# The opening of a two-network fp32 kernel: modulation by four column chunks, the first two value heads in plain fp32

## The chip, the cores and the metric

One core of a Trainium2 chip runs the kernel. The metric is the device time of one execution in microseconds (us), median of several runs. The engines are TensorE (PE), VectorE (DVE), ScalarE (ACT), GpSimd (POOL) and SyncE (SP), which here issues all transfers.

## What is computed

Two small networks of two layers each, 512 tokens by 1024 features in fp32. The change touches only the start of the first layer:

```
cond = silu(c)
mod = cond @ ada_w[l] + ada_b[l]
shift, scale, gate = split(mod, 3)
h = x * (1 + scale) + shift
proj = h @ w_in                       # u, v, z_a, x_b, z_b, 1024 columns each
v = layer_norm(v per head of 256 columns, norm_g, norm_b)
sv = einsum('hts,bnshd->bnthd', masked ws, v)   # "spatial" product, per head
a = u * (sv + b) * silu(z_a)
...                                   # pooling branch, output product, three more layers
```

## The kernel before

The weights `wt` lie in tiles T of 128 by 2048 numbers (1 MB). ACT rounds a tile to fp32r (`w_hi`, `split_tile`), DVE takes the rest (`w_lo`), and every large product is three fp32r matmuls (`mm3`: low by high, high by low, high by high). The modulated input is split in the same way into `h_hi` and `h_lo`, eight blocks k of 128 features. Tiles T = 0 to 3 are the value heads h = 0 to 3 ("V"), each in two chunks of one PSUM bank (c = 0, 1, two token blocks each); T = 4 and on are U, Z, ZB, XB and the rest. For each V chunk ACT copies the bank to `tmp`, and DVE normalizes it into `vn` ("post": statistics, reciprocal, scaling). `spatial(h)` multiplies `vn` of head h by `ws` into banks 4 and 5, from which DVE makes `park`; the next spatial product may only overwrite a bank when `park` of the one before has been read out of it (`sv_taken`).

A unit is one of shift, scale, gate of a layer. Its columns are the sum over eight pieces k (128 rows of `adat`, 1024 columns, 512 KB each) of `cond[k]` times the piece, which DVE adds up in `acc`; PE then sums over the partitions by multiplying with `ones`, one column a matmul. In the opening, units 0 (shift) and 1 (scale) are needed before `h` exists. All 16 pieces, `ada_first`, are fetched first, pieces 1 and 3 go straight through PE (`first_mods`, L1024), and scale is done in two halves. `keep_busy` multiplies constants for no result. `wb[T]` is the weight buffer of a tile, `before_in[T]` the tile that was in it. One pair of buffers takes all tiles but three.

All orders are written out by hand: `plan_steps` makes one list of steps, each engine walks it, and counting semaphores tie them. SP issues transfers in its own order and waits where a buffer is in use. DVE also adds a piece of a later unit (`ada_piece`) in each tile, fetched into `ada_raw` by halves of 64 rows.

## Time and profile before

| | |
|---|---|
| median of 3 runs | 1363.78 us (1362.84 to 1364.08) |
| the profiled execution | 1363.42 us |
| its span | 1361.6 us |
| PE busy | 1327.5 us, 97% of the span |
| DVE busy | 912.9 us, 67% |
| ACT busy | 563.5 us, 41% |

The span is what the trace covers; the execution's time is 1.8 us more. Busy time of PE is modelled for pipelined matmuls, so it tells where PE has work, not how fast it is.

### The profile page before, as it was taken

What the parts mean: (1) busy time and instruction counts of PE and PEld (TensorE: products, weight loads), DVE (VectorE), ACT (ScalarE), POOL (GpSimd) and SP (SyncE); (2) the same over time, 40 slices, a digit from 0 to 9 for tenths busy, and PEclk for the clock granted to TensorE, in tenths of its full rate; (3) what the DMA queues carried; (4) which work ended last, traced back from release to release, by engine and by line L of the source; (5) the groups of instructions that cost most, each with busy time, mean ns of one, the idle gap of its engine ahead of it and who ended that gap; (6) DMA issues with size and microseconds to landing.
All of it is one profiled execution on the core that took longest, in us unless ns stands there. A gap on an engine that the chain in (4) does not pass through costs nothing.

```text
span 1361.6 us, 17379 instructions
## 1 busy us (share of the span) xinstructions
PE 1327.5 (97%) x6761; PEld 1123.4 (83%) x6761; DVE 912.9 (67%) x1325; ACT 563.5 (41%) x851; POOL 303.3 (22%) x204
## 2 busy tenths in 40 slices
PE   5999999999999999999999999999999999999997
PEld 5998888778888878888888788888888888888885
DVE  5754544774486568988678786686776577676553
ACT  1423222221254246666422475543342566534430
POOL 0200200064420015555344100001116200011123
PEclk9999999999999999999999999999999999999998
DMA  9654443323424422213344243313314322211111
GB/s 378 187 165 139 139 140 141 136 94 139 147 93 140 132 74 63 70 36 93 94 139 140 93 158 118 96 48 139 135 51 161 118 93 78 78 63 62 62 63 62
DMA packets 31378, 155.14 MB, mean 114 GB/s; under 512 B 4160, under 2 KB 4288, under 8 KB 20032
## 3 DMA queue, kind: packets, MB, share of 16 engines
q1 hardware_dynamic: 31296, 154.03, 33.5%
q8 instruction: 54, 0.88, 0.3%
q14 instruction: 28, 0.23, 0.1%
HBM read 151.92 MB, written 2.10 MB: 113 GB/s over the span
## 4 chain that ended last, share of the span: by engine, by line
PE 87%; DVE 6%; issue 3%; ACT 3%; DMA 1%; SPq 0%; POOL 0%; DVEq 0%; ACTq 0%; POOLq 0%
PE bank L838 25%; PE bank L840 24%; PE bank L839 24%; PE bank L845 1%; PE bank L1302 1%; PE bank L992 1%; PE bank L1136 1%; PE bank L1276 1%; DVE acc L1669 1%; PE bank L1278 1%; PE bank L974 1%; DMA ada_first<-adat 1%; PE bank L1123 1%; PE bank L1140 1%; DVE qn_lo L1928 1%
## 5 line engine op out<-in xcount | busy, mean ns | idle before, releaser
L838 PE MATMUL bank<-h_lo,w_hi 128*128 128x512 f32 x1008 | 397.5, 394 | 1.5 <-DVE h_lo L1805 1.0
L840 PE MATMUL bank<-h_hi,w_hi 128*128 128x512 f32 x1008 | 392.8, 390 | 0.0
L839 PE MATMUL bank<-h_hi,w_lo 128*128 128x512 f32 x1008 | 392.4, 389 | 0.0
L1628 DVE TENSOR_TENSOR w_lo<-w_raw,w_hi 128x2048 fp32r<-128x2048 f32 (+2 forms) x91 | 207.1, 2276 | 85.6 <-ACT w_hi L1347 85.5
L838 PEld LDWEIGHTS bank<-h_lo,w_hi 128*128 128x128 f32 x1008 | 189.3, 188 | 41.1 <-issue 3.5
L840 PEld LDWEIGHTS bank<-h_hi,w_hi 128*128 128x128 f32 x1008 | 189.2, 188 | 40.0
L839 PEld LDWEIGHTS bank<-h_hi,w_lo 128*128 128x128 f32 x1008 | 189.4, 188 | 38.2 <-issue 0.5
L1347 ACT ACTIVATE w_hi<-w_raw 128x2048 fp32r<-128x2048 f32 (+2 forms) x91 | 166.7, 1832 | 86.0 <-PE bank L840 77.8
L1423 ACT ACTIVATE tmp<-bank 128x512 f32<-128x512 f32 x48 | 28.6, 595 | 124.4 <-PE bank L840 115.0
L2214 POOL TENSOR_SCALAR q_dup<-rot_y 128x512 fp32r<-128x512 f32 x8 | 11.9, 1492 | 302.7 <-DVE rot_y L1680 302.7
L1669 DVE SCALAR_TENSOR_TENSOR acc<-ada_raw,cond_pair,acc 128x1024 f32<-128x1024 f32 x45 | 58.5, 1300 | 0.0
L838 PE MATMUL bank<-mixc_lo,w_hi 128*128 128x512 f32 x128 | 50.6, 396 | 0.0
L840 PE MATMUL bank<-mixc_hi,w_hi 128*128 128x512 f32 x128 | 49.9, 390 | 0.0
L839 PE MATMUL bank<-mixc_hi,w_lo 128*128 128x512 f32 x128 | 49.8, 389 | 0.0
L2128 DVE TENSOR_TENSOR_SCAN keep<-keep 128x127 f32<-128x127 f32 (+2 forms) x64 | 49.0, 807 | 0.4
L2227 POOL TENSOR_TENSOR sum<-sum,sqr 128x512 f32<-128x512 f32 x24 | 48.0, 2001 | 1.9
L1764 DVE SCALAR_TENSOR_TENSOR x<-bank,gate,x 128x512 f32<-128x512 f32 x16 | 12.0, 751 | 50.5 <-PE bank L840 50.4
L2305 POOL TENSOR_TENSOR rope_t<-qr_f,sin 32x512 f32<-32x512 f32 x28 | 37.9, 1353 | 33.2 <-ACT qr_f L1562 30.7
L2226 POOL TENSOR_TENSOR sqr<-x 128x512 f32<-128x512 f32 x24 | 37.5, 1560 | 23.8 <-DVE x L1774 22.7
L1669 DVE SCALAR_TENSOR_TENSOR acc<-ada_raw,cond,acc 128x1024 f32<-128x1024 f32 x28 | 41.1, 1469 | 0.0
L2214 POOL TENSOR_SCALAR mixc_hi<-sz 128x512 fp32r<-128x512 f32 x16 | 23.9, 1492 | 76.0 <-DVE sz L1914 76.0
L2214 POOL TENSOR_SCALAR mixa_hi<-park 128x512 fp32r<-128x512 f32 x8 | 11.9, 1492 | 124.4 <-DVE park L1737 124.4
(349 smaller groups left out, 2675.0 us busy)
## 6 DMA issues: line engine op xcount, KB each, us to landing
w_raw<-wt SPq DMA_DIRECT2D x83, 1024.0 KB, 6.0
ada_raw<-adat SPq DMA_DIRECT2D x96, 256.0 KB, 4.0
ada_raw<-adat SPq DMA_DIRECT2D x32, 512.0 KB, 3.6
ada_first<-adat SPq DMA_DIRECT2D x16, 512.0 KB, 12.4
w_raw<-wt SPq DMA_DIRECT2D x8, 640.0 KB, 5.2
spare_raw<-wt SPq DMA_DIRECT2D x3, 1024.0 KB, 5.9
x<-xt SPq DMA_DIRECT2D x4, 512.0 KB, 15.5
out<-outf SPq DMA_DIRECT2D x8, 256.0 KB, 2.2
```

What stands on the lines that cost most here:

```text
L838: pe.matmul(dst, ah, bl, start=start, stop=False, skip_group_check=True)
L839: pe.matmul(dst, al, bh, start=False, stop=False, skip_group_check=True)
L840: return pe.matmul(dst, ah, bh, start=False, stop=stop, skip_group_check=True)
L1347: act.activation(w_hi[wb[T]][:, 0:n], w_raw[wb[T]][:, 0:n], ACT.Copy).then_inc(w_hi_done, 1)
L1423: act.activation(dst, src, func, scale=scale, bias=bias).then_inc(chunk_taken, 1)
L1628: dve.tensor_tensor(w_lo[wb[T]][:, 0:n], w_raw[wb[T]][:, 0:n], f(w_hi[wb[T]][:, 0:n]), ALU.subtract).then_inc(w_lo_done, 1)
L1669: dve.scalar_tensor_tensor(acc[:, g % 2, :], src, c, acc[:, g % 2, :], ALU.mult, ALU.add).then_inc(ada_done, 1)
L2128: ins = dve.tensor_tensor_scan(k, k, k, 1.0, ALU.mult, ALU.min)
L2214: return pool.tensor_scalar(dst, src, 1.0, None, ALU.mult)
L2226: link(pool.tensor_tensor(sqr[:], x[:, n, :], x[:, n, :], ALU.mult))
L2227: ins = pool.tensor_tensor(sum2[:], sum2[:], sqr[:], ALU.add)
L2305: pool.tensor_tensor(rope_t[to, :], qr_f[of, :], sin1[of, :], ALU.mult).then_inc(qr_turned, 1)
```

## The change

The two units of the opening are fetched by four chunks of 256 columns each, both units in one transfer: 32 pieces of 256 KB in place of 16 of 512 KB. After each chunk DVE and PE make the columns of two blocks k, ACT makes `h_first` (plain fp32) and from it `h_hi`, and PE multiplies the two blocks for value heads 0 and 1 at once in fp32, with the weights as they landed (`first_values`; four banks, one for each chunk of output). So tiles 0 and 1 are not split. Tiles 2 and 3 land in buffers of their own (`early_raw`). The direct pieces, `keep_busy` in the opening and POOL's copy of `h` go. The spatial product of head 0 moves from behind head 1 to between the two chunks of head 2, that of head 1 stays behind head 2. `splits(T)` counts the split tiles, in place of T + 1 everywhere. The diff, cut to its core:

```diff
--- before.py
+++ after.py
@@ -139,10 +139,12 @@
     for h in range(GH):
         T = begin()
         chunk("V", T, h=h, c=0)
+        if h == 2:
+            steps.append(dict(op="spatial", h=0))
         chunk("V", T, h=h, c=1)
         if h == 0:
             steps.append(dict(op="spatial_rows"))
-        else:
+        elif h >= 2:
             steps.append(dict(op="spatial", h=h - 1))
         after_tile(T)
...
@@ -478,6 +488,9 @@
             w_hi.append(place(f"spare_hi{i}", [P, TILE], F32R, o + 8 * KB))
             w_lo.append(place(f"spare_lo{i}", [P, TILE], F32R, o + 16 * KB))
+        for i in range(2):
+            w_raw.append(place(f"early_raw{i}", [P, TILE], F32, area + (16 + 8 * i) * KB))
...
@@ -698,6 +714,8 @@
         def split_with(T):
+            if T < 3:
+                return [3] if T == 1 else []
...
@@ -739,6 +757,8 @@
         for d in kinds:
             aside = d["kind"] in ("AV", "AG") and d["u"] == 0 or d["kind"] == "QC" and d["n"] >= 2 or d.get("aside")
             bk = CHUNK_BANK[d["C"]] = (2 + d.get("sub", 0)) if aside else 2 if d is OUT0_FIRST else d["C"] % 2
+            if d["C"] in OPENING:
+                bk = CHUNK_BANK[d["C"]] = d["C"]
             BEFORE_IN_BANK[d["C"]] = last_in.get(bk, -1)
...
@@ -775,20 +795,39 @@
         @block.sync
         def _(sp):
             sp.dma_start(cols[:], colst).then_inc(cols_in, 16)
-            sp.dma_start(w_raw[0][:], wt[0]).then_inc(w_landed[0], 16)
-            for i in range(2 * SEC):
-                sp.dma_start(ada_first[:, i, :], adat[i]).then_inc(ada_first_landed[i], 16)
-                if i == 0:
-                    sp.dma_start(mats[:], matst).then_inc(const_in, 16)
-                    sp.dma_start(rmats_raw[:], rmatst).then_inc(rmats_in, 16)
-            for i in range(4):
+            def first_chunk(c):
+                for k in range(SEC):
+                    cut = slice(FIRST_COLS * c, FIRST_COLS * (c + 1))
+                    sp.dma_start(ada_first[:, c, k], adat[k:SEC + k + 1:SEC, :, cut].rearrange("u p d -> p u d")
+                                 ).then_inc(ada_first_landed[SEC * c + k], 16)
+            def first_x(i):
                 sp.dma_start(x[:, 2 * i:2 * i + 2, :], xt[:, 2 * i:2 * i + 2, :]).then_inc(x_landed[i], 16)
-            sp.dma_start(w_raw[1][:], wt[1]).then_inc(w_landed[1], 16)
+            def first_weights(T):
+                sp.dma_start(w_raw[raw_of[T]][:], wt[T]).then_inc(w_landed[raw_of[T]], 16)
+            first_chunk(0)
+            sp.dma_start(mats[:], matst).then_inc(const_in, 16)
+            first_weights(0)
+            first_x(0)
+            first_weights(1)
+            for c in range(1, FIRST_CHUNKS):
+                first_chunk(c)
+                if c == FIRST_CHUNKS - 1:
+                    sp.wait_ge(ada_done, 2 * SEC)
+                    first_weights(2)
+                first_x(c)
             sp.dma_start(ws[:], wst).then_inc(layer0_in, 16)
             sp.dma_start(bs[:], bst).then_inc(layer0_in, 16)
+            sp.dma_start(rmats_raw[:], rmatst).then_inc(rmats_in, 16)
+            first_weights(3)
             for T in range(NT):
-                if before_in[T] >= 0:
-                    sp.wait_ge(w_lo_done, before_in[T] + 1)
+                if raw_before[T] >= 2:
+                    sp.wait_ge(w_lo_done, splits(raw_before[T]))
+                elif raw_before[T] >= 0:
+                    wait_tile_done(sp, raw_before[T])
                 if 2 <= before_in[T] - head_tile <= MH // 2:
                     sp.wait_ge(uv_lo_done, before_in[T] - head_tile - 1)
                 if T == spare_tiles[0]:
@@ -799,8 +838,8 @@
                 elif T == spare_tiles[2]:
                     sp.wait_ge(ro_full, RH)
                 n = cols_of[T]
-                if T >= 2:
-                    sp.dma_start(w_raw[wb[T]][:, 0:n], wt[T, :, 0:n]).then_inc(w_landed[wb[T]], 16)
+                if T >= 4:
...
@@ -1015,37 +1035,49 @@
                                   h_hi[:, k, :], h_lo[:, k, :], i == 0, i == DC - 1)
                 ins.then_inc(chunk_full, 1)
...
+            def first_columns(c):
+                pe.wait_ge(ada_done, SEC * (c + 1))
+                if c >= 2:
+                    pe.wait_ge(first_cols, c - 1)
+                for u in range(2):
+                    for j in range(FIRST_COLS // P):
+                        a = FIRST_COLS * c + P * j
+                        i = u * FIRST_COLS // P + j
+                        ins = pe.matmul(bank[:, 6 + c % 2, i:i + 1], acc[:, u, a:a + P], ones[:, 0:1],
+                                        start=True, stop=True)
+                ins.then_inc(first_full, 1)
+            def first_values(k, h):
+                pe.wait_ge(h_v_done, k + 1)
+                if k == 0:
+                    pe.wait_ge(w_landed[raw_of[h]], 16)
+                for c in range(2):
+                    for i in range(2):
+                        blk = slice((2 * c + i) * P, (2 * c + i + 1) * P)
+                        ins = pe.matmul(bank[:, 2 * h + c, i * HD:(i + 1) * HD], h_first[:, k, blk],
+                                        w_raw[raw_of[h]][:, k * HD:(k + 1) * HD], start=i == 0 and k == 0,
+                                        stop=k == DC - 1, skip_group_check=True)
+                    if k == DC - 1:
+                        ins.then_inc(chunk_full, 1)
+            def opening():
                 pe.wait_ge(const_in, 16)
...
+                first_columns(0)
+                for k in range(DC):
+                    first_values(k, 0)
+                    if k in (3, 5):
+                        first_columns((k + 1) // 2)
+                    first_values(k, 1)
+                    if k == 1:
+                        first_columns(1)
             def head_qr(j):
                 T = head_tile + j
...
+                pe.wait_ge(w_lo_done, splits(T))
                 if j == 0:
                     pe.wait_ge(qk_lo, 4)
                 if j == 1:
...
@@ -1424,14 +1458,11 @@
             act.wait_ge(cols_in, 16)
             act.activation(cond[:], col("c", 0, 16), ACT.Silu).then_inc(cond_done, 1)
-            split_tile(0)
             act.wait_ge(cond_done, 1)
             for e in range(2):
                 for i in range(2):
                     act.activation(cond_pair[64 * e:64 * e + 64, :, i], cond[64 * i:64 * i + 64, :],
                                    ACT.Copy).then_inc(cond_pair_done, 1)
-            act.wait_ge(rmats_in, 16)
-            act.activation(rmats[:].rearrange("p a b -> p (a b)"), rmats_raw[:], ACT.Copy).then_inc(masks_done, 1)
             v_count = 0
             for d in steps:
                 op = d["op"]
@@ -1454,11 +1485,20 @@
                                    bias=eps_ln[:] if d["mean"] else eps_rho[:] if d["lhs"] == "derived" else
                                    col("eps", d["eps"])).then_inc(sts_done, 1)
                 elif op == "h" and d["l"] == 0:
-                    for k in range(DC):
-                        act.wait_ge(first_cols, k // 4 + 1)
-                        act.wait_ge(x_landed[k // 2], 16)
-                        act.activation(h_hi[:, k, :], x[:, k, :], ACT.Identity, scale=h_scale[:, 0, k:k + 1],
-                                       bias=h_shift[:, 0, k:k + 1]).then_inc(h_hi_done, 1)
+                    for c in range(FIRST_CHUNKS):
+                        if c == FIRST_CHUNKS - 1:
+                            split_tile(2)
+                        act.wait_ge(first_cols, c + 1)
+                        act.wait_ge(x_landed[c], 16)
+                        for k in (2 * c, 2 * c + 1):
+                            act.activation(h_first[:, k, :], x[:, k, :], ACT.Identity, scale=h_scale[:, 0, k:k + 1],
+                                           bias=h_shift[:, 0, k:k + 1]).then_inc(h_v_done, 1)
+                        for k in (2 * c, 2 * c + 1):
+                            act.wait_ge(h_v_done, k + 1)
+                            act.activation(h_hi[:, k, :], h_first[:, k, :], ACT.Copy).then_inc(h_hi_done, 1)
+                    act.wait_ge(rmats_in, 16)
+                    act.activation(rmats[:].rearrange("p a b -> p (a b)"), rmats_raw[:],
+                                   ACT.Copy).then_inc(masks_done, 1)
                 elif op == "ln" or op == "h":
                     l = d["l"]
                     first = H_T_BASE[op, l]
...
@@ -1818,15 +1850,37 @@
                     link(dve.tensor_copy(h_shift[:, l, :], shift))
                 dve.tensor_tensor(h_scale[:, l, :], h_scale[:, l, :], gain, ALU.mult).then_inc(cols_done, 1)
...
+            def first_sum(c, k):
+                dve.wait_ge(ada_first_landed[SEC * c + k], 16)
+                cut = slice(FIRST_COLS * c, FIRST_COLS * (c + 1))
+                if k == 0:
+                    ins = dve.tensor_scalar(acc[:, :, cut], ada_first[:, c, k], cond[:, k:k + 1], None, ALU.mult)
+                else:
+                    dve.wait_ge(ada_done, SEC * c + k)
+                    ins = dve.scalar_tensor_tensor(acc[:, :, cut], ada_first[:, c, k], cond[:, k:k + 1],
+                                                   acc[:, :, cut], ALU.mult, ALU.add)
+                ins.then_inc(ada_done, 1)
+            def first_columns(c):
+                dve.wait_ge(first_full, c + 1)
+                n = FIRST_COLS // P
+                j = slice(n * c, n * (c + 1))
+                dve.tensor_tensor(h_shift[:, 0, j], bank[:, 6 + c % 2, 0:n], col("ada_b", n * c, n), ALU.add)
+                dve.scalar_tensor_tensor(h_scale[:, 0, j], bank[:, 6 + c % 2, n:2 * n], 1.0,
+                                         col("ada_b", DC + n * c, n), ALU.add, ALU.add).then_inc(first_cols, 1)
+            def opening():
+                for k in range(SEC):
+                    first_sum(0, k)
+                first_columns(0)
+                for c in range(1, FIRST_CHUNKS):
+                    for k in range(SEC):
+                        first_sum(c, k)
+                        if c >= 2 and k == c - 2:
+                            first_columns(c - 1)
             def statistics(d):
                 si, w = d["stat"], 1.0 / d["width"]
...
@@ -1957,9 +2011,6 @@
             dve.wait_ge(cond_done, 1)
             dve.tensor_scalar(eps_ln[:], col("eps", 0), 1.0 / ALPHA ** 2, None, ALU.mult)
-            split_tile(0)
-            for q in range(2 * SEC):
-                ada_piece(q)
             for d in steps:
                 op = d["op"]
                 if op == "tile":
@@ -2007,9 +2058,12 @@
                     if "T" in d:
                         ada_piece(d["T"] + 2 * SEC)
                 elif op == "h" and d["l"] == 0:
-                    first_columns()
+                    opening()
                     for k in range(DC):
+                        if k == 2:
+                            first_columns(FIRST_CHUNKS - 1)
                         h_low(0, k)
+                    split_tile(2)
                     dve.wait_ge(layer0_in, 32)
                     dve.memset(ws[64:P, :, 0:64], 0.0).then_inc(ws_done, 1)
...
```

SP, from the start of its program (the names are destination and source). Before:

```order
L777 DMA cols<-colst 128x197
L778 DMA w_raw_84<-wt 128x2048
L780 DMA ada_first<-adat 128x1024
L782 DMA mats<-matst 128x576
L783 DMA rmats_raw<-rmatst 128x512
L780 DMA ada_first<-adat 128x1024 x15
L785 DMA x<-xt 128x1024 x4
L786 DMA w_raw_85<-wt 128x2048
```

Now:

```order
L797 DMA cols<-colst 128x197
L802 DMA ada_first<-adat 128x2x256 x8
L812 DMA mats<-matst 128x576
L809 DMA w_raw_84<-wt 128x2048
L806 DMA x<-xt 128x1024
L809 DMA w_raw_85<-wt 128x2048
L802 DMA ada_first<-adat 128x2x256 x8
L806 DMA x<-xt 128x1024
L802 DMA ada_first<-adat 128x2x256 x8
L806 DMA x<-xt 128x1024
L802 DMA ada_first<-adat 128x2x256 x8
L809 DMA early_raw_185<-wt 128x2048 [waits ada_done]
```

The last two blocks of `x` and tile 3 follow behind the last row. The weights of heads 0, 1 and 2 now all stand ahead of the last block of `x`; before, only those of head 0 did.

DVE, from the end of the opening to the `park` of head 0. Before, with the posts of heads 0 and 1 as they follow `w_lo` of tile 1:

```order
L1628 TENSOR_TENSOR w_lo_89<-w_raw_85,w_hi_87 128x2048
L1661 TENSOR_SCALAR acc<-ada_raw,cond_pair 128x1024
...
L1987 SCALAR_TENSOR_TENSOR rb<-bank,cols,bs 128x128 x8
L1628 TENSOR_TENSOR w_lo_88<-w_raw_84,w_hi_86 128x2048
L1669 SCALAR_TENSOR_TENSOR acc<-ada_raw,cond_pair,acc 128x1024
...
L1997 SCALAR_TENSOR_TENSOR park<-bank,cols,rb 128x512 x2
```

Now the `park` of head 0 stands behind one more chunk of posts, that of head 2, and one more piece:

```order
43 L1837 TENSOR_TENSOR h_lo<-h_first,h_hi 128x512 [waits h_v_done,h_hi_done] x6
44 L1668 TENSOR_TENSOR w_lo_88<-early_raw_185,w_hi_86 128x2048 [waits w_hi_done]
45 L2069 MEMSET ws 64x4x64 [waits layer0_in]
46 L1697 TENSOR_SCALAR acc<-ada_raw,cond_pair 128x1024 [waits first_full,cond_pair_done,ada_landed0]
...
63 L1668 TENSOR_TENSOR w_lo_89<-early_raw_186,w_hi_87 128x2048 [waits w_hi_done]
64 L1700 SCALAR_TENSOR_TENSOR acc<-ada_raw,cond_pair,acc 128x1024 [waits ada_done,ada_landed1]
...
79 L1700 SCALAR_TENSOR_TENSOR acc<-ada_raw,cond_pair,acc 128x1024 [waits ada_done,ada_landed0]
...
87 L2048 SCALAR_TENSOR_TENSOR park<-bank,cols,rb 128x512 [waits sv_full,rb_done]
```

Between rows 46 and 63 stand the posts of head 0 and `rb`, between 64 and 79 those of head 1, between 79 and 87 that of chunk 0 of head 2. On every engine the rows from tile 4 on are the same as before but for the numbers of lines.

## Rows read from the trace of the kernel before

**Rows 1.** Windows: busy time of each engine, granted clock, DMA share, GB/s.

```profile
11.00:34.00 23.00, 20.36 (x91) 18.43 (x91) 18.08 (x20) 1.84 (x3) 1.76 (x2) 1.00 1.03 413
34.00:86.50 52.50, 52.50 (x435) 52.00 (x436) 37.22 (x81) 19.26 (x27) 7.93 (x7) 1.00 0.64 198
```

**Rows 2.** Timeline of PE up to head 0 (start, us, engine, line, count, idle before).

```profile
11.16 6.96 PE L1024 MATMUL bank<-cond,ada_first 128*128 128x1 f32 x32 [11.16 <-DMA ada_first<-adat]
20.49 3.55 PE L1029 MATMUL bank<-mats,acc 128*128 128x1 f32 x16 [2.37 <-DVE acc L1669]
23.90 7.24 PE L845 MATMUL bank<-rmats 128*128 128x512 f32 x22
30.98 1.84 PE L1040 MATMUL bank<-mats,acc 128*128 128x1 f32 x16
33.95 0.35 PE L838 MATMUL bank<-w_lo,h_hi 128*128 128x256 f32 x1
```

**Rows 3.** PE between the heads: rows product, spatial products, the matmul after one.

```profile
45.53 1.02 PE L1161 MATMUL bank<-ws,mats 128*128 128x512 f32 x2
57.90 1.95 PE L1172 MATMUL bank<-ws,vn 128*128 128x128 f32 x16
...
71.20 1.95 PE L1172 MATMUL bank<-ws,vn 128*128 128x128 f32 x16
73.22 0.28 PE L840 MATMUL bank<-w_hi,h_hi 128*128 128x256 f32 x1
```

**Rows 4.** Timeline of SP: the issues of the opening.

```profile
3.55 11.32 SPq L780 DMA_DIRECT2D ada_first<-adat  x15
14.91 4.45 SPq L785 DMA_DIRECT2D x<-xt  x4
19.41 0.43 SPq L786 DMA_DIRECT2D w_raw<-wt  x1
27.41 0.58 SPq L803 DMA_DIRECT2D w_raw<-wt  x1
```

**Rows 5.** From issue to landing: ada_first, x, w_raw of head 1, w_raw of later tiles.

```profile
L780 SPq DMA_DIRECT2D ada_first<-adat x16: 424/474/2907, 1.6 to 13.8; - x16
DMA to landing us min/median/max: 6.7/12.4/16.6
...
DMA to landing us min/median/max: 15.3/15.5/15.8
...
DMA to landing us min/median/max: 17.2/17.2/17.2
...
DMA to landing us min/median/max: 4.8/5.9/18.2
```

**Rows 6.** DMA queue: packets, MB, share of 16 engines; 12 to 27 us, and 1354 to 1361.6.

```profile
q1 hardware_dynamic: 1690, 6.16, 102.9%
...
q1 hardware_dynamic: 1152, 2.10, 74.6%
```

**Rows 7.** Timeline of DVE: the sums of the opening, and what follows them.

```profile
19.06 1.28 DVE L1669 SCALAR_TENSOR_TENSOR acc<-ada_first,cond,acc 128x1024 f32<-128x1024 f32 x1
29.62 1.41 DVE L1665 SCALAR_TENSOR_TENSOR acc<-ada_first,cond,acc 128x512 f32<-128x512 f32 x2
...
42.84 0.27 DVE L2015 MEMSET ws<- 64x256 f32 x1
43.14 2.29 DVE L1628 TENSOR_TENSOR w_lo<-w_raw,w_hi 128x2048 fp32r<-128x2048 f32 x1
45.35 0.75 DVE L1661 TENSOR_SCALAR acc<-ada_raw,cond_pair 128x1024 f32<-128x1024 f32 x1
46.02 0.74 DVE L1719 BATCH_NORM_STATS2 v_stats<-tmp 128x6 f32<-128x256 f32 x2
48.45 0.86 DVE L1719 BATCH_NORM_STATS2 v_stats<-tmp 128x6 f32<-128x256 f32 x2
50.80 2.16 DVE L1987 SCALAR_TENSOR_TENSOR rb<-bank,cols,bs 128x128 f32<-128x128 f32 x8
52.87 2.28 DVE L1628 TENSOR_TENSOR w_lo<-w_raw,w_hi 128x2048 fp32r<-128x2048 f32 x1
56.27 0.74 DVE L1719 BATCH_NORM_STATS2 v_stats<-tmp 128x6 f32<-128x256 f32 x2
58.73 0.75 DVE L1719 BATCH_NORM_STATS2 v_stats<-tmp 128x6 f32<-128x256 f32 x2
60.98 1.41 DVE L1997 SCALAR_TENSOR_TENSOR park<-bank,cols,rb 128x512 f32<-128x512 f32 x2
```

**Rows 8.** Timeline of ACT in the opening.

```profile
32.16 5.76 ACT L1460 ACTIVATE h_hi<-x,h_shift,h_scale 128x512 fp32r<-128x512 f32 x8 [21.78 <-DVE h_scale L1828]
37.83 1.90 ACT L1347 ACTIVATE w_hi<-w_raw 128x2048 fp32r<-128x2048 f32 x1
```

**Rows 9.** fp32 matmuls of 384, 256 and 128 columns, and the start of the next.

```profile
565.10 1.46 PE L1136 MATMUL bank<-pT,v_tok 128*128 128x384 f32 x6
566.40 1.06 PE L1140 MATMUL bank<-pT,v_tok 128*128 128x128 f32 x8
```

**Rows 10.** Windows around 369 us, where the granted clock falls.

```profile
366.00:369.40 3.40, 3.40 (x29) 3.24 (x28) 0.75 (x1) 1.67 (x2) 0.00 (x0) 1.00 0.60 189
369.40:376.20 6.80, 6.80 (x25) 5.79 (x25) 3.04 (x14) 0.54 (x2) 0.00 (x0) 0.50 0.48 176
```

More of the change, by code:

```diff
@@ L314, in build @@
     NT = totals["T"]
-    wb, before_in, landed, last_tile = [], [], [], {}
+    wb, before_in, last_tile = [], [], {}
     for T in range(NT):
@@ L319, in build @@
         before_in.append(last_tile.get(kind, -1))
-        landed.append(16 + (landed[before_in[T]] if kind in last_tile else 0))
-        last_tile[kind] = T
+        if T >= 2:
+            last_tile[kind] = T
+    raw_of, raw_before, landed, last_raw = [], [], [], {}
+    for T in range(NT):
+        kind = 3 + T if T in (2, 3) else wb[T]
+        raw_of.append(kind)
+        raw_before.append(last_raw.get(kind, -1))
+        landed.append(16 + (landed[raw_before[T]] if kind in last_raw else 0))
+        last_raw[kind] = T
     cols_of = {T: HEAD_COLS if head_tile <= T < head_tile + MH // 2 else TILE for T in range(NT)}
@@ L393, in build @@
         KB = 1024
[L396 removed]
+        ada_first = place("ada_first", [P, FIRST_CHUNKS, SEC, 2, FIRST_COLS], F32, area)
+        h_first = place("h_first", [P, DC, S], F32, area)
         vn = place("vn", [P, 2, NB, HD], F32, area)
@@ L501, in build @@
         decay_in = sem("decay_in")
-        w_landed = [sem(f"w_landed{i}") for i in range(5)]
+        w_landed = [sem(f"w_landed{i}") for i in range(7)]
         w_hi_done = sem("w_hi_done")
@@ L507, in build @@
         ada_landed = [sem(f"ada_landed{i}") for i in range(2)]
-        ada_first_landed = [sem(f"ada_first_landed{i}") for i in range(16)]
+        ada_first_landed = [sem(f"ada_first_landed{i}") for i in range(FIRST_CHUNKS * SEC)]
         ada_done = sem("ada_done")
@@ L646, in pieces_summed, with splits @@
         def pieces_summed(q):
-            return q - sum(i < q for i in DIRECT_PIECES)
+            return q - 2 * SEC + FIRST_CHUNKS * SEC
+        def splits(T):
+            return T - 1
         piece_at = {}
@@ L724, in build @@
         AG_CHUNK = {d["g"]: d["C"] for d in kinds if d["kind"] == "AG"}
-        PAIRED = {d["C"] for d in kinds if (d["kind"], d.get("h"), d.get("c")) == ("V", 0, 0)}
+        OPENING = {d["C"] for d in kinds if d["kind"] == "V" and d["h"] < 2}
         FOURS = {d["C"]: kinds[i:i + 4] for i, d in enumerate(kinds) if (d["kind"], d.get("n", d.get("u"))) in
@@ L855, in _ @@
             layer = [0]
-            def chunk_pair(d):
-                T, C = d["T"], d["C"]
-                for c in range(2):
-                    wait_taken(pe, BEFORE_IN_BANK[C + c])
-                for k in range(DC):
-                    wait_h(layer[0], k)
-                    for c in range(2):
-                        dst = bank[:, (C + c) % 2, :]
-                        for i in range(2):
-                            blk = slice((2 * c + i) * P, (2 * c + i + 1) * P)
-                            w = slice(k * HD, (k + 1) * HD)
-                            ins = mm3(dst[:, i * HD:(i + 1) * HD], h_hi[:, k, blk], h_lo[:, k, blk],
-                                      w_hi[wb[T]][:, w], w_lo[wb[T]][:, w], i == 0 and k == 0, k == DC - 1)
-                        if k == DC - 1:
-                            ins.then_inc(chunk_full, 1)
             def chunk_four(four):
@@ L1338, in split_tile @@
                 n = early_columns(T)
-                act.wait_ge(w_landed[wb[T]], landed[T])
+                act.wait_ge(w_landed[raw_of[T]], landed[T])
                 j = T - head_tile
```

97 lines of the change are left out of this document (23 added, 74 removed).

## The prediction

> **What bounds the kernel now.** I read the windows first [rows 1]. From 34.0 us on PE is busy throughout (52.50 of 52.50 us), and the page gives it 97% of the span; so the whole change is decided by when PE gets through heads 0 to 3, and by what it waits for on the way. From 11 to 34 us the queue moves 413 GB/s at a share of 1.03: the transfers are the bound there. The timeline of PE shows what it did meanwhile [rows 2]: single-column matmuls and 22 constant ones (L845), none of which is work that the result must wait for; the first matmul of head 0 starts at 33.95 us. From there PE runs head 0 until the rows product at 45.53 and, later, a spatial product (2.0 us each, from 71.20 to 73.22) between heads of 11.3 us (57.90 + 2.0 to 71.20) [rows 3]. Head 3 starts at 73.2, so tile 4 starts at 73.2 + 11.3 + 2.0 = 86.5 us. From tile 4 on all engines have the same rows in the same order in both kernels, and PE is full before and after; the gain or loss is therefore 86.5 minus the new start of tile 4.
>
> **The transfers, reconstructed from before.** The last block of x landed at 18.3 + 15.8 = 34.1 us, the weights of head 1 at 19.4 + 17.2 = 36.6, 2.5 us later [rows 4, 5]. Four blocks of x of 512 KB landed between 14.9 + 15.3 = 30.2 and 34.1, one in 1.28 us. So before the last block the queue had 16 pieces at 1.28 (20.4), one tile at 2.5, the two constants (0.54 MB at 413 GB/s, 1.4) and four blocks (5.1), 29.4 us, and an origin of 34.1 - 29.4 = 4.7 us. The first piece at 1.6 + 6.7 = 8.3 fits: 4.7 + 2.5 + 1.28 = 8.5.
>
> Now the last block of x stands behind 32 pieces of P us each, one constant (0.8), three tiles (7.5) and with the four blocks (5.1): it lands at 4.7 + 13.4 + 32 P = 18.1 + 32 P. Nothing in the trace has rows of 1 KB, which the new pieces have. A 4 KB row takes 1.28/8 = 160 ns on one of 16 engines, one of 8 KB 2.5/8 = 313: 38 ns for a KB and 7 for the row, so 45 ns for 1 KB and 16 x 45 = 0.72 us a piece. The rows of 2 KB at the end of the kernel took 0.746 x 7.6 x 16 / 1024 = 89 ns [rows 6]; 38 less is 51 ns, P = 0.81. These are the bounds; I take 0.75, nearer to the loads than to the stores. The last x lands at 42.1 us, 8 us later than before.
>
> The Trainium skill, "DMA: Bandwidth & Descriptors" (section Why small descriptors are slow), puts the extra cost of a packet at about 3 cycles beside one for each 32 bytes. By that 1 KB would take 38 x 35/32 = 42 ns, P would be 0.67, and the sum 1358.4 us; the rows here show more for a row than that (7 to 13 ns, not 4), so I stay with them.
>
> **The change on the path.** DVE sums a piece of 512 columns in 0.7 us (half of the 1.41 of L1665 [rows 7]), just under P, so it keeps up. Tile 2 lands one block before the last x, at 40.8; ACT rounds it first (1.9 us, to 42.7), then makes blocks 6 and 7 at 0.72 each (5.76/8 [rows 8]) to 44.1, and rounds them, not in the trace, priced alike at 0.7, to 45.6. DVE: last `h_lo` 0.7, to 46.3; `w_lo` of tile 2 2.2 (43.14 to 45.35), to 48.5; memset 0.3, to 48.8 [rows 7]. The first `ada_raw` piece is behind ws, bs and rmats (0.65 each, 1.9), tile 3 (2.5) and two halves: from 34.1 to 27.4 + 18.2 = 45.6 the old queue had two tiles, ws, bs and four halves [rows 4, 5], so (11.5 - 5.0 - 1.3)/4 = 1.3 a half. It lands at 42.1 + 1.9 + 2.5 + 2.6 = 49.1 and is summed at 49.8. Then one chain on DVE, all prices from [rows 7]: posts of head 0 4.8 (46.02 to 50.80), 54.6; `rb` 2.1, 56.7; `w_lo` of tile 3 and a piece 3.4 (52.87 to 56.27), 60.1; posts of head 1, 2.25 each where nothing waits (58.73 to 60.98), 64.6; a piece 1.2, 65.8; post of head 2 chunk 0, 68.05; first `park` 0.7, 68.8.
>
> PE: an fp32 matmul of 256 columns takes a third of the 1.30 us from 565.10 to 566.40 for 768 columns [rows 9], 0.433 us; a block of one head (four) 1.73. In all 64 of them, 27.7 us, for 23 us of split matmuls. Blocks 6 and 7 of both heads run from 43.4 to 50.4; rows product 0.9; head 2 chunk 0 to 57.0; spatial(0) (its `rb` is there at 56.7) to 59.0; chunk 1 to 64.6. Then spatial(1) finds bank 4 unread until `park` at 68.8: a **new wait of 4.2 us**, with head 3 and all later tiles queued behind it. It takes 2.0, head 3 11.3, spatial(2) 2.0: tile 4 starts at 84.1, **2.4 us earlier** than 86.5. The same number from the other side: heads 0 and 1 and the rows product are done at 51.3 in place of 57.9, 6.6 us earlier, and the wait takes 4.2 of them, since DVE now has two heads of posts at once where it had 11 us of matmuls beside each.
>
> Nothing for the following, with what hides it: PE's extra 4.5 us and the eight-record column sums (0.9 each) lie under the transfers. In detail, x block 0 is there at 15.3, PE starts at 16.0, the first block at half clock (L1024 took 0.217 us a record against 0.115 for L1040 [rows 2], so the clock was at its lower level, 1.2 GHz, in the old opening until the constant matmuls had run); with waits of 1.7 us before block 2, PE ends block 5 at 43.1, 0.3 us before block 6 is there. Behind that it may be 1.2 us late before the posts of head 0 feel it (first bank full at 48.0, needed by 49.2). ACT's 16 operations in place of 8 lie under the transfers too; POOL's copy of h served only `h_lo`, and goes; rmats is used by nothing in this stretch.
>
> **The sum.** 1363.4 (profiled execution; 0.4 under the median) - 2.4 = 1361.0 us.
>
> **The rivals.**
> - *SP or the queue takes a piece at a fixed cost* (slower). A piece now has two source runs a partition. SP issued one old piece in 0.47 us (median), but x at 4.45/4 = 1.1 each [rows 4, 5]. If two runs cost twice 0.45, P = 0.9 and the last x is 4.8 us later: tile 4 at 88.9, 1365.8. At 1.1, 11.2 later: 1372.2. It decides from P = 0.825. Against: the 1.1 comes when some dozen transfers are under way, about the pace of landing, and a tile of the same number of rows was issued in 0.43 behind it. 14%.
> - *The clock of PE falls in the gaps.* Between 366.0 and 369.4 us PE ran mostly single-column matmuls, and the granted clock was 0.50 for the next 6.8 us [rows 10]. At 25.6 us the new order has four such matmuls and a wait of 1.7 us. One fall of 3.4 to 6.8 us costs 1.7 to 3.4, less 1.5 of slack: 1361.2 to 1362.9. 15%. Falls at each chunk cost 5 to 10: 1364.5 to 1369.5. 6%. The Trainium skill, "TensorE: Matmul & The Clock Gate" (section HAM oscillation), says that bursts of matmuls with waits for transfers between them fall back each time; the trace agrees that it falls in such a stretch, and no row has bursts like these.
> - *The two units' reads get in each other's way.* They lie 4 MB apart in memory, and each engine goes to and fro between them. If they halve the rate, P = 1.5, the last x is 24 us later: 1385. 3%; the blocks of x are rows with a pitch of their own and came at full rate. [...]
> - *The chain is shorter* (more gain). P at 0.71 or less, copies at 0.6, posts without idle: the wait goes to 2 us, gain 4 to 6, 1357.4 to 1359.4. 12%.
> - *As summed*, 50%, own range 1359.8 to 1362.4 from P = 0.72 (1.0 sooner) to P = 0.79 (1.3 later).
>
> **Chances.** A measurement of this kernel can tell about 0.2%, 2.7 us. Faster by more: the short chain and four tenths of the likeliest, 0.33. Within: 0.45. Slower: issue, repeated clock falls, memory, 0.22. The range 1357.5 to 1367.0 leaves out the upper part of the issue case (9%), the memory case (3%), the worst clock (2%) and gains over 6 us (4%).
>
> **What would show it.** Right: pieces landing 0.75 us apart, the last x near 42, a PE wait of some 4 us before L1205 for DVE `park`, tile 4 near 84. Wrong: SP issues over 0.8 us each with a queue not full; a granted clock of 0.50 between 20 and 50 us; no wait at spatial(1), or PE waits inside head 2 for `w_lo` or `h_lo`.

## The result, and the profile after

The changed kernel takes 1367.59 us (median of 16 runs), the kernel before 1363.69 in the same session (median of 16): ratio 1.0022, 95% interval 1.0014 to 1.0029, so about 3 us slower by the ratio. A second session with the same two kernels gave 1.0016 [1.0007, 1.0025]. The forecast was 1361.0 with a range up to 1367.0: wrong in sign, and outside the range by 0.6 us. (The ratio is not the quotient of the two medians, which would be 1.0029, or 3.9 us; all runs of both kernels were in the fast state.)

The profiled execution of the changed kernel took 1367.65 us, its span is 1365.8 us (before: 1361.6). First the windows (columns as in [rows 1]): the opening, the stretch up to the start of tile 4, and three short ones inside it.

```profile
11.00:34.00 23.00, 17.53 (x65) 14.93 (x66) 13.57 (x23) 5.12 (x8) 0.00 (x0) 0.93 1.06 372
34.00:89.10 55.10, 50.98 (x340) 48.27 (x339) 40.89 (x93) 18.77 (x29) 0.00 (x0) 0.94 0.67 218
...
28.80:32.20 3.40, 3.40 (x9) 2.66 (x10) 2.98 (x5) 1.52 (x3) 0.00 (x0) 0.50 1.07 370
69.80:76.50 6.70, 5.16 (x24) 5.18 (x25) 5.88 (x14) 2.35 (x3) 0.00 (x0) 0.50 0.97 339
499.90:503.10 3.20, 3.20 (x9) 2.42 (x9) 0.93 (x5) 1.09 (x4) 0.00 (x0) 0.50 0.00 0
```

Against [rows 1] two things are new. PE is no longer full behind 34 us: 50.98 of 55.10. And the granted clock is not 1.00 there: it reads 0.50, which is 1.2 in place of 2.4 GHz, at 29 us, for the whole stretch from 69.8 to 76.5 us, and once more at 500 us. What PE waited for up to 140 us (engine, line, for whom; us in total, times, longest):

```profile
PE bank L1047 <- DVE acc L1861: 13.1, 1, 13.1
PE bank L1205 <- DVE park L2048: 4.1, 1, 4.1
PE bank L1059 <- ACT h_first L1494: 3.4, 2, 2.2
```

The second line is the forecast wait at spatial(1), 4.1 us for 4.2. The timeline of PE around it, the last line being spatial(2), behind which tile 4 starts:

```profile
43.40 0.95 PE L1047 MATMUL bank<-mats,acc 128*128 128x1 f32 x8
44.21 8.88 PE L1059 MATMUL bank<-w_raw,h_first 128*128 128x256 f32 x40
52.93 1.02 PE L1194 MATMUL bank<-ws,mats 128*128 128x512 f32 x2
...
71.34 3.76 PE L1205 MATMUL bank<-ws,vn 128*128 128x128 f32 x16 [4.12 <-DVE park L2048]
...
87.14 1.95 PE L1205 MATMUL bank<-ws,vn 128*128 128x128 f32 x16
```

The same 16 matmuls take 1.95 us in [rows 3] and at 87.14, and 3.76 at 71.34: spatial(1) runs at half clock, since the clock fell while PE was waiting for `park`. Tile 4 starts at 87.14 + 1.95 = 89.1 us; forecast 84.1, before 86.5.

The timeline of DVE tells why `park` was late itself, beside [rows 7]:

```profile
48.14 2.29 DVE L1668 TENSOR_TENSOR w_lo<-early_raw,w_hi 128x2048 fp32r<-128x2048 f32 x1
50.53 0.27 DVE L2069 MEMSET ws<- 64x256 f32 x1
51.52 0.75 DVE L1697 TENSOR_SCALAR acc<-ada_raw,cond_pair 128x1024 f32<-128x1024 f32 x1 [0.71 <-DMA ada_raw<-adat]
52.19 0.74 DVE L1750 BATCH_NORM_STATS2 v_stats<-tmp 128x6 f32<-128x256 f32 x2
...
70.45 1.40 DVE L2048 SCALAR_TENSOR_TENSOR park<-bank,cols,rb 128x512 f32<-128x512 f32 x2
...
95.25 0.69 DVE L1765 TENSOR_TENSOR park<-park,tmp 128x512 f32<-128x512 f32 x1 [0.22 <-ACT tmp L1457]
```

The chain from the end of the first `ada_raw` sum (52.2) to the end of the first of the two `park` operations (70.45 + 0.70 = 71.15) is 19.0 us, as added up; but it starts at 52.2, not at 49.8. The last row, the post of the first U chunk in tile 4, serves as a mark below: its work is the same in all kernels. Before it stood at 92.60 (then L1734):

```profile
92.60 0.69 DVE L1734 TENSOR_TENSOR park<-park,tmp 128x512 f32<-128x512 f32 x1 [0.22 <-ACT tmp L1423]
```

So 2.65 us of the loss are there at the mark, and about 3 is what the runs show. The issues of SP, beside [rows 4], were as hoped: 0.50 us (4.01/8) for a piece while the queue had room, later at the queue's own pace (6.21/8 and 6.10/8, 0.77):

```profile
1.16 4.01 SPq L802 DMA_DIRECT2D ada_first<-adat  x8
...
19.05 6.21 SPq L802 DMA_DIRECT2D ada_first<-adat  x8
25.30 0.96 SPq L806 DMA_DIRECT2D x<-xt  x1
26.31 6.10 SPq L802 DMA_DIRECT2D ada_first<-adat  x8
32.45 1.08 SPq L809 DMA_DIRECT2D early_raw<-wt  x1
33.57 0.43 SPq L806 DMA_DIRECT2D x<-xt  x1
```

The last x, issued at 33.57, took 9.5 us to landing: 43.1, for a forecast of 42.1.

### The profile page after: what moved, and what is told of

It is laid out like the page before. It is cut to its first block, busy times and chain, and to the rows that moved or that the text cites. A ratio compares the mean times of both kernels' runs of the same rounds, so it can differ in the third digit from the quotient of the medians.

```text
span 1365.8 us, 17174 instructions
## 1 busy us (share of the span) xinstructions
PE 1325.0 (97%) x6639; PEld 1117.3 (82%) x6639; DVE 913.4 (67%) x1345; ACT 563.7 (41%) x857; POOL 293.6 (21%) x196
## 4 chain that ended last, share of the span: by engine, by line
PE 83%; DVE 8%; issue 4%; ACT 3%; DMA 2%; SPq 1%; POOL 0%; DVEq 0%; ACTq 0%; POOLq 0%
PE bank L877 24%; PE bank L879 23%; PE bank L878 23%; PE bank L1336 1%; DMA ada_raw<-adat 1%; PE bank L1012 1%; PE bank L1310 1%; PE bank L1168 1%; PE bank L1312 1%; PE bank L994 1%; DMA x<-xt 1%; PE bank L1059 1%; DVE qn_lo L1982 1%; ACT p_even L1559 1%; DVE acc L1700 1%
## 5 line engine op out<-in xcount | busy, mean ns | idle before, releaser
L1668 DVE TENSOR_TENSOR w_lo<-w_raw,w_hi 128x2048 fp32r<-128x2048 f32 (+2 forms) x87 | 198.0, 2276 | 81.2 <-ACT w_hi L1381 81.1
L1381 ACT ACTIVATE w_hi<-w_raw 128x2048 fp32r<-128x2048 f32 (+2 forms) x87 | 159.1, 1829 | 83.3 <-PE bank L879 77.8
L878 PE MATMUL bank<-mixc_hi,w_lo 128*128 128x512 f32 x128 | 49.8, 389 | 0.0
L2268 POOL TENSOR_SCALAR mixc_hi<-sz 128x512 fp32r<-128x512 f32 x16 | 23.9, 1491 | 76.1 <-DVE sz L1968 76.1
```

The source lines that it names most:

```text
L878: pe.matmul(dst, al, bh, start=False, stop=False, skip_group_check=True)
L1381: act.activation(w_hi[wb[T]][:, 0:n], w_raw[raw_of[T]][:, 0:n], ACT.Copy).then_inc(w_hi_done, 1)
L1668: dve.tensor_tensor(w_lo[wb[T]][:, 0:n], w_raw[raw_of[T]][:, 0:n], f(w_hi[wb[T]][:, 0:n]), ALU.subtract).then_inc(w_lo_done, 1)
L2268: return pool.tensor_scalar(dst, src, 1.0, None, ALU.mult)
```

## The experiments

Two theories. **A:** the granted clock falls in the new wait, and spatial(1) and a part of head 3 at half clock cost some 2.6 us on top of the wait; the wait of 4.1 us itself is the forecast price. **B:** wait and late transfers carry the loss alone, and the fall is harmless. All numbers together; "first park" and "mark" are starts in DVE's timeline (mark: first post of a U chunk), "lower" is the length of the stretch at 0.50 in and behind that wait (a fall elsewhere is not in this column). All experiments but "before, new order" are edits of the changed kernel. They ran in three sessions, in which the kernel before had medians of 1364.69 us (wait filled, parks first, old order, spatial(1) moved), 1364.90 (once more; before, new order; piece early; moved, parks, piece) and 1364.44 (the other four); so the ratio compares kernels of different sessions better than the median. The last four columns come from one trace each.

| kernel | median us | ratio to before | longest wait at a spatial product | lower | first park | mark |
|---|---|---|---|---|---|---|
| before | - | 1 | none | - | 60.98 | 92.60 |
| changed | 1367.59 | 1.0022 [1.0014, 1.0029] | 4.1 | 6.8 | 70.45 | 95.25 |
| changed, once more | 1365.92 | 1.0016 [1.0007, 1.0025] | 4.1 | 6.8 | 70.62 | 95.52 |
| wait filled with matmuls | 1364.16 | 0.9997 [0.9986, 1.0008] | 0.9 | none | 71.54 | 93.84 |
| DVE parks first | 1363.34 | 0.9997 [0.9985, 1.0009] | 2.2 | none | 67.91 | 90.28 |
| old order | 1367.37 | 1.0024 [1.0013, 1.0036] | 6.8 | 6.8 | 67.60 | 96.90 |
| before, new order | 1363.65 | 0.9999 [0.9988, 1.0011] | none | none | 67.89 | 92.91 |
| piece early | 1366.33 | 1.0017 [1.0008, 1.0027] | 3.6 | 3.4 | 69.95 | 93.89 |
| last x first | 1367.22 | 1.0015 [1.0005, 1.0026] | 4.5 | 6.8 | 70.17 | 94.55 |
| spatial(1) moved | 1362.33 | 0.9983 [0.9971, 0.9995] | 1.2 | none | 70.22 | 89.44 |
| moved, parks, piece | 1360.74 | 0.9971 [0.9960, 0.9982] | none | none | 69.97 | 91.04 |
| **moved, parks** | 1359.31 | 0.9958 [0.9946, 0.9969] | 0.4 | none | 67.13 | 88.21 |
| moved, parks, x | 1359.80 | 0.9968 [0.9957, 0.9979] | 1.3 | none | 67.96 | 89.03 |
| moved, parks, x, piece | 1360.24 | 0.9956 [0.9941, 0.9971] | none | none | 68.61 | 89.68 |

**The changed kernel once more.** No edit.

> The changed kernel once more, unaltered, beside the others of this group, with a second profile. Theory A expects the wait of about 4 us at spatial(1) again and a stretch at half clock in or behind it in this execution too, and a time of 1367 to 1368. If the clock stays up at 70 us and the time is the same as before, the fall is not what costs.

Windows of this second trace:

```profile
66.00:70.00 4.00, 1.41 (x12) 1.21 (x11) 3.21 (x10) 1.34 (x4) 0.00 (x0) 1.00 0.68 245
70.20:76.90 6.70, 5.39 (x25) 5.42 (x26) 5.89 (x14) 2.11 (x3) 0.00 (x0) 0.50 0.93 333
```

PE is busy 1.41 of 4.00 us, and then at half clock. The same wait, the same fall at the same place: it belongs to the kernel. The time was 1365.9, a little under what was expected, but the ratio is again slower.

**The wait filled.** Ahead of spatial(1) on PE:

```
if h == 1:
    pe.wait_ge(masks_done, 1)
    keep_busy(16, 6)      # bank 6: nobody reads it
```

> The changed kernel with 16 constant matmuls (128x512, written to a bank that nobody reads) put on PE ahead of spatial(1), where it now waits 4.1 us for park. Theory A (the granted clock falls in that wait, and spatial(1) and half of head 3 then run at the lower level): the clock stays at 1.00 there, tile 4 starts at about 71.2 + 2.0 + 11.3 + 2.0 = 86.5 in place of 89.1 us, and the time is 2.6 us lower, about 1365.0. Theory B (the wait and the later pieces alone carry the loss, the fall is harmless): the time stays at 1367.6. If the clock falls anyway or later, likewise 1367.6.

Timeline of PE (the constant matmuls carry the mark "rmats", here L884), and its windows:

```profile
68.24 3.92 PE L884 MATMUL bank<-rmats 128*128 128x512 f32 x16 [0.28 <-DVE vn L1764]
72.34 2.05 PE L1208 MATMUL bank<-ws,vn 128*128 128x128 f32 x16 [0.18 <-DVE park L2051]
...
71.50:78.30 6.80, 6.62 (x54) 6.16 (x54) 6.37 (x13) 2.10 (x2) 0.00 (x0) 1.00 0.96 337
```

No useful work is begun sooner; spatial(1) starts 1.0 us later than in the changed kernel (72.34 for 71.34), because the transfers were later in this execution. Yet the mark comes 1.4 us earlier, and the ratio goes from 1.0016 or 1.0022 to 0.9997: 2.6 to 3.4 us. From the first park to the mark the time is 22.3 us here and 24.8 in the changed kernel: 2.5 us is the price of the fall. It lies between the starts of spatial(1) and spatial(2), 13.4 us here (72.34 to 85.74) and 15.8 in the changed kernel (71.34 to 87.14). B expected no change and is out: the interval lies below that of the first session of the changed kernel and just touches that of the second (1.0008 and 1.0007), and the two traces differ by the whole 2.5 us. In this trace too the clock fell in the opening (0.50 for 3.4 us from 28 us on), so that fall is not what makes the difference.

**DVE parks first.** In DVE's program alone, the two `park` operations of spatial(0) stand ahead of the post of head 2 chunk 0:

```
 elif op == "chunk":
+    if (d["kind"], d.get("h"), d.get("c")) == ("V", 2, 0):
+        park_spatial(0)
     chunk(d)
```

> The changed kernel with DVE alone in another order: the two park operations of spatial(0) ahead of the post of head 2 chunk 0 (2.4 us), so that the wait at spatial(1) is about 1.8 in place of 4.1 us. Theory B (a wait costs its length): 2.3 us less, 1365.3. Theory A with a shorter wait too short to bring the clock down: another 2.6 less, 1362.7, and a granted clock of 1.00 from 66 to 80 us.

The wait is 2.2 us, the windows read 1.00 throughout, and from the first park to the mark it is 22.4 us, as in the filled kernel:

```profile
63.00:67.90 4.90, 3.57 (x30) 3.37 (x29) 3.96 (x12) 1.56 (x4) 0.00 (x0) 1.00 0.89 249
67.90:76.00 8.10, 7.20 (x61) 7.23 (x62) 7.13 (x20) 2.88 (x4) 0.00 (x0) 1.00 0.95 342
```

The mark is 5.0 us before that of the changed kernel: 2.5 from the first park, 2.5 from the clock. In the medians it is 4.3 or 2.6 (1363.3 for 1367.6 and 1365.9) and in the ratios 2.6 to 3.4, less than the trace has: the profiled execution (1361.7) was one of the short ones, and the ratio alone does not tell this kernel from the filled one. The median lies between the numbers of A (1362.7) and B (1365.3), nearer to A; it is the trace that decides.

**The old order.** The new opening, with spatial(0) behind head 1 and spatial(1) behind head 2 as before.

```
-        if h == 2:
-            steps.append(dict(op="spatial", h=0))
         chunk("V", T, h=h, c=1)
 ...
-        elif h >= 2:
+        elif h >= 1:
             steps.append(dict(op="spatial", h=h - 1))
```

> The changed kernel with the old places of the spatial products (spatial(0) behind head 1, spatial(1) behind head 2); the new opening alone. PE is done with the rows product at about 53 and waits for the last rb at 59.0 (6 us), spatial(0) to 61, head 2 to 72.3, spatial(1) to 74.3, head 3 and spatial(2) to 87.6: without a fall of the clock in that wait 1.5 us under the changed kernel, 1366.1; with one of 6.8 us at half level (about 2.6 to 3.4 us) 1368.7 to 1369.5. So theory A expects the slower number, theory B the lower.

```profile
52.00:58.00 6.00, 0.82 (x2) 0.00 (x0) 4.93 (x18) 2.51 (x4) 0.00 (x0) 1.00 0.34 89
58.20:64.90 6.70, 5.25 (x24) 5.25 (x25) 6.27 (x15) 1.42 (x4) 0.00 (x0) 0.50 0.09 12
```

The wait is 6.8 us, now for `rb`, and the clock falls in it. The median of 1367.4 is between the two numbers expected; the mark at 96.90, 1.6 us behind that of the changed kernel, is that of the slower one. So the new opening brings nothing by itself in either of these two orders: wherever the spatial product stands, PE comes to it before DVE has done two heads' posts.

**The new order in the kernel before.** The two lines of the same edit in the old kernel.

> The kernel before with the new places of the spatial products alone (spatial(0) between the chunks of head 2, none behind head 1); the old opening. Its heads have their posts 11 us apart, so park(0) is done by about 68 us, ahead of spatial(1) at 71.2, and all sums of work on PE are the same: no new wait and no change, within 0.5 us of before. Rival (the new order costs by itself, a wait at spatial(1) here too): 2 us or more above before.

0.9999, as expected, and a mark at 92.91. The order costs and brings nothing where DVE has 11 us for each head; with the last experiment this puts the loss on the new opening.

**The first piece early.** The first `ada_raw` piece right behind the last x on SP's queue:

```
+            modulation_piece(0)
             sp.dma_start(ws[:], wst).then_inc(layer0_in, 16)
             sp.dma_start(bs[:], bst).then_inc(layer0_in, 16)
```

> The changed kernel with one transfer moved: the first ada_raw piece is issued right behind the last x, ahead of ws, bs, rmats and tile 3, so that it lands near 46 in place of 51.5 us. If the late piece is what starts the DVE chain late, the chain begins at the end of the memset (50.8, or 49.5 when w_lo of tile 2 is not late itself), and the wait at spatial(1) falls from 4.1 by 0.7 to 2.0 us: 1365.6 to 1366.9 by the wait's length alone (theory B), 1363.0 to 1364.3 if the shorter wait keeps the clock up too (theory A). If the piece does not matter, the wait and 1367.6 stay.

DVE no longer waits for the piece, but its chain starts only 0.5 us earlier (51.01 for 51.52), bound by `w_lo` of tile 2; the wait at spatial(1) is 0.5 us shorter, where at least 0.7 was expected, and the clock still falls, for 3.4 us, here only at 71.7, when spatial(1) has started (70.84). From the first park to the mark it is 23.9 us, between 22.3 without a fall and 24.8 with one of 6.8. The ratio does not differ from that of the changed kernel, though the mark of this one trace is 1.4 us earlier. Why `w_lo` of tile 2 was late is told by ACT, which makes blocks 6 and 7; the changed kernel first, then this one, and the window of the fall:

```profile
44.65 1.52 ACT L1494 ACTIVATE h_first<-x,h_shift,h_scale 128x512 f32<-128x512 f32 x2 [0.91 <-DVE h_scale L1871]
```

```profile
45.03 1.52 ACT L1499 ACTIVATE h_first<-x,h_shift,h_scale 128x512 f32<-128x512 f32 x2 [0.29 <-DMA x<-xt]
...
71.70:75.00 3.30, 3.30 (x18) 3.30 (x17) 2.87 (x9) 2.10 (x2) 0.00 (x0) 0.50 0.91 326
```

The changed kernel waited for the columns of the last chunk (`h_scale`), which PE made late because the clock had fallen in the opening; `w_lo` started at 48.14. Here the clock stayed up in the opening, but the last x landed late, and `w_lo` started at 48.31. In the four traces with neither (parks first, old order, moved, moved with parks) it started at 46.2 to 47.2. The issue-to-landing times of the last x, here first in this kernel, then in the one that combines it with the moved product:

```profile
DMA to landing us min/median/max: 12.0/12.0/12.0
```

```profile
DMA to landing us min/median/max: 13.0/13.0/13.0
```

It was 9.5 in both traces of the changed kernel, and 9.6 to 11.0 in the five other kernels whose queues are the same. The x was issued first, and yet it came latest in the two kernels with the piece right behind it. That a transfer pulled forward takes from the one in front of it is the likely reading, from one trace of each kernel.

**The last x first.** The last x ahead of tile 2 on the queue, and ACT's rounding of tile 2 behind blocks 6 and 7.

```
+                first_x(c)
-                if c == FIRST_CHUNKS - 1:
-                    sp.wait_ge(ada_done, 2 * SEC)
-                    first_weights(2)
-                first_x(c)
+            sp.wait_ge(ada_done, 2 * SEC)
+            first_weights(2)
```

> The changed kernel with the last block of x ahead of tile 2 on SP's queue, and ACT's rounding of tile 2 behind the copies of blocks 6 and 7. The last x lands at about 40.8 in place of 43.1 us. If the late x is what costs (its landing was 1.0 us behind the forecast), PE starts blocks 6 and 7 earlier and the time falls by up to 1 us. Against: the columns of the last chunk are only made at 44.4, because PE is busy with the blocks before until 43.4, and DVE's chain starts from w_lo of tile 2 and the ada_raw piece, which move by nothing or are later; then it stays at 1366 to 1367.6.

```profile
DMA to landing us min/median/max: 8.2/8.2/8.2
```

The x is there at 40.0, 3 us sooner, and nothing comes of it: wait 4.5, clock at 0.50, 1.0015. DVE had `w_lo` of tile 2 and the memset behind it at 49.6 and waited for the first `ada_raw` piece until 51.2. So the late x is not on the path here, and the piece is what starts the chain.

**spatial(1) moved.** In the plan:

```
-        if h == 2:
-            steps.append(dict(op="spatial", h=0))
+        if h >= 2:
+            steps.append(dict(op="spatial", h=h - 2))
         chunk("V", T, h=h, c=1)
 ...
-        elif h >= 2:
-            steps.append(dict(op="spatial", h=h - 1))
+        elif h == 3:
+            steps.append(dict(op="spatial", h=2))
```

> The changed kernel with spatial(1) moved behind chunk 0 of head 3, so that PE has 5.6 us of matmuls to do while DVE gets to park. If wait and fall are the loss (theories A and B both): PE runs head 3 chunk 0 from 67.0 to 72.6, spatial(1) to 74.6, chunk 1 to 80.2, spatial(2) after a wait of about 0.5 us for the second park to 82.7; tile 4 starts 6.4 us before 89.1, and the time is 1361.2. Rival (the DVE chain, which the late piece of the modulation starts, is the bound and only moves the wait on): a wait of 3 us or more at spatial(2), the time 1364 or more.

```profile
72.34 1.95 PE L1205 MATMUL bank<-ws,vn 128*128 128x128 f32 x16
81.26 2.02 PE L1205 MATMUL bank<-ws,vn 128*128 128x128 f32 x16 [1.22 <-DVE park L2048]
```

With the first park at the same time as in the changed kernel (70.22), spatial(1) waits for nothing, the clock stays up, and the mark comes 5.8 us earlier. 1.2 us of wait are left at spatial(2). The median of 1362.3 is 1.1 us over the number expected and under the rival's 1364. The kernel beats the one before: 0.9983, with an interval just under 1.

**spatial(1) moved and parks first.** The last edit, and in DVE's program the park of spatial(h - 2) ahead of the post of head h, chunk 0 (h = 2 and 3).

> The best kernel so far without its transfer part: spatial(1) behind chunk 0 of head 3, and DVE's park of spatial(0) and spatial(1) ahead of the posts. In the combined kernel's trace the last x landed 2.8 us later than in the changed one and PE waited 2.8 us for it, so the early ada_raw piece took away about what it gave. If that is so, this one is equal to or below the combined one (1360.7): 1360 to 1361. If the early piece is worth 0.7 us or more: 1361.4 or above.

Waits of PE from 50 to 140 us, and the window from 53 to 83 us:

```profile
PE bank L1205 <- DVE rb L2053: 0.4, 1, 0.4
```

```profile
53.00:83.00 30.00, 29.57 (x241) 28.92 (x240) 25.68 (x67) 8.98 (x16) 0.00 (x0) 1.00 0.63 188
```

PE is full again, as in [rows 1]. Mark 88.21, 4.4 us before that of the kernel before and 7.0 before the changed one; 0.9958 [0.9946, 0.9969], from five runs. It has the lowest median of all, 5.7 us faster than before by its ratio and 4.1 by the spans of the two traces (1357.5 for 1361.6). 1360 to 1361 or more was expected; it lies at or under the combined kernel, so the early piece brings nothing that these runs can show.

**All of it, and two more.** The combination with the early piece, and both with the last x first:

> A candidate to beat both: the changed kernel with spatial(1) behind chunk 0 of head 3, DVE's park of spatial(0) and spatial(1) ahead of the posts of the chunk in front of which they stand, and the first ada_raw piece right behind the last x. Against the kernel with spatial(1) moved alone it takes away the wait of 1.2 us at spatial(2) for park and the one of 0.7 us at spatial(0) for rb: 1.2 to 1.9 us less than the moved one, about 3.5 to 4.3 us less than before. If these waits turn into others, as much as the moved one (2.4 us less than before).

> As e8_moved_parks, with the last x ahead of tile 2 as well. With the wait at spatial(1) gone PE is bound by its own work from 28 us on, so an x that lands before 43 us can't bring more than 0.3 us; what it takes away is the case in which the last x lands late (45 us and more): equal to e8_moved_parks in the median, at most 0.5 us lower.

> The combined kernel with the last x ahead of tile 2: now the ada_raw piece can't hold the last x up. If holding x up was the price of the early piece, 1 to 2 us less than the combined one (1358.7 to 1359.7); else the same 1360.7.

1360.7, 1359.8 and 1360.2: none is told apart from the plain moved version with parks, whose interval theirs overlap. The combined kernel is 4.0 us faster than before by its ratio, as expected (3.5 to 4.3). In its trace PE waited 2.8 us for block 6, until 46.79, with the last x landing at 45.8, as the 13.0 us above say, and the clock fell behind this wait too:

```profile
47.80:51.00 3.20, 3.20 (x9) 2.54 (x8) 3.01 (x3) 1.31 (x3) 0.00 (x0) 0.50 0.97 284
```

Whether the x ahead of tile 2 takes that away for good stays open; the last kernel's median, of six runs in another session, is 0.5 us lower, where 1 to 2 was expected.

## Why the prediction was wrong

- **Issue and pace of the pieces: right.** 0.50 us an issue, a queue pace of 0.77 for P = 0.75; neither the fixed cost of an issue nor memory conflicts showed. By the extra cost of a packet in the Trainium skill, "DMA: Bandwidth & Descriptors" (section Why small descriptors are slow), the prediction's estimate of P was 0.67; the trace does not agree, and the higher price taken from the rows was nearer.
- **The wait at spatial(1): right in place and length** (4.1 for 4.2), and the chain of 19.0 us on DVE to the tenth. That the length came out is luck in part, since both its ends were late alike and for different reasons: PE reached spatial(1) at 67.2 for 64.6, DVE's first park was done at 71.15 for 68.8. With PE on time the wait would have been 6.5 us and the end the same (an estimate from these starts).
- **The step that failed: "It takes 2.0, head 3 11.3", said of spatial(1) behind the wait.** These prices are those of [rows 3], at a granted clock of 1.00. The rival on the clock looked for falls "in the gaps" of the opening alone, and gave them 1.5 us of slack; the forecast's own new gap of 4.2 us, with everything queued behind it, was never held against [rows 10]. It measured: 3.76 us for 1.95, and 2.5 us in all up to the mark (24.8 for 22.3 without the fall). The Trainium skill, "TensorE: Matmul & The Clock Gate" (section HAM oscillation), tells of bursts of matmuls with waits for transfers between them, in which the clock falls back each time. The prediction cited it for the gaps of the opening alone. The traces show the same of a wait for another engine: down in both traces of the changed kernel, and up in the one with the wait filled. [rows 10], which the prediction set beside the page, are no case of a wait: PE had work in all 3.40 us ahead of that fall.
- **The second term that failed, of the same size: the first `ada_raw` piece at 49.1.** DVE waited for it until 51.5, 2.4 us more: 1.0 from the last x (0.6 of it by the pace of 0.77 over 32 pieces, an estimate), the rest behind it, for which no run shows the reason. This went into the end one for one, since it starts the chain. With either term alone wrong the sum would have been about 1363.4, no gain; only both together turn it into a loss. It is not the piece alone: `w_lo` of tile 2 was done at 50.4 for 48.5, mostly because of the fall in the opening, and without the wait for the piece the chain started only 0.5 us earlier.
- **The fall in the opening came too, and was hidden.** At 28.8 to 32.2 us the clock was at 0.50 in both traces of the changed kernel; of the twelve traces with the new opening four have this fall. PE was done with heads 0 and 1 at 52.9 there; in the kernel with spatial(1) moved, where it did not fall, at 51.4, and DVE's chain started at 51.5 and at 51.3. But the 1.5 us of slack were not what hid it: the first bank was copied out by ACT from 50.54 on, where the prediction needed it full by 49.2. It was the late piece that held the chain back longer. The prediction's reading that PE starts at its lower level held: eight single-column records take 1.83 us at 13.1 and 0.95 at 26.5, though the windows read 1.00 for both.
- **The sum again:** -2.4, +2.35 (first park at 70.45 for 68.1), +2.5 (clock) gives +2.45 at the mark; measured +2.65. The span has +4.2, since from the mark to the end there are 1270.5 us for 1269.0. No run lays this rest to the change: in the other kernels the same stretch took 1267.7 (wait filled) to 1271.2 (moved). The falls of the clock behind the mark do not give it either: the one near 500 us is also in the trace of the old opening with the new order, where this stretch took 1268.8, and all together they last 18.2 us in the trace of before and 17.5 in that of the changed kernel. Its cause stays open. The medians, +3.9 and +1.0 us, and the ratios, +3.0 and +2.2, lie around 2.65.

Open: why the pieces behind the last x took longer than summed. No experiment parts the transfers behind it from one another.

## What to carry to other kernels

A wait on PE can have two prices, its length and what the clock takes from the work behind it (here 4.1 us and 2.5 us); price both for every wait that a forecast itself puts in. Follow a fall to the other engines too: the one in the opening made `w_lo` of tile 2 on DVE 1 to 2 us later (48.14 for 46.2 to 47.2). If the producer is late by a known amount, put independent matmuls in front of the waiting product: one chunk moved took away 5.8 us where filling with constants took away about 2.5. And if an opening makes one engine faster, look how many rounds of work the next engine then gets at once: the gain ended on DVE, whose posts had 11 us each before and now had to do two heads in a row.

## What was not expected of the hardware

- The fall is no chance event of one execution: 6.8 us at 0.50 at 69.8 and at 70.1 us in the two traces of the changed kernel, 6.8 in those with waits of 6.8 and 4.5 us, 3.4 in those with 3.6 us and (for block 6, in the combined kernel) 2.8 us; none with a wait of 2.2 us or with the wait filled. Other falls vary while the instructions stay: at 492 to 502 us, behind 16 single-column matmuls, twelve of the fourteen traces have 3.4 us at 0.50, the kernel before and the filled one have none. At 369 us before has 6.8 us and the changed kernel 3.4; near 758 us it is the other way round. The row of before in the window of the last row of the first fence above; its own 16 single-column matmuls stand at 493.7, and nowhere from 486 to 506 us does it read less than 1.00:

```profile
499.90:503.10 3.20, 3.20 (x16) 2.77 (x16) 2.19 (x6) 1.43 (x5) 2.87 (x2) 1.00 0.00 0
```

- A transfer issued on the same queue behind another one can delay it: the last x took 9.5 to 11.0 us to landing with ws behind it (seven traces), 12.0 and 13.0 with two 64-partition halves of `ada_raw` behind it; ahead of tile 2 it took 8.2 and 8.5, and 10.2 with those halves behind tile 2. The five traces with changed queues agree, with one or two of each.
